# First block: the relative-bias table laid out outside the kernel and loaded once, in place of 64 one-hot products and seven copies

## The reference

```python
bias = rpb[:, dr[None, None, :, None], dc[:, :, None, :]].astype(jnp.float32)
s_loc = jnp.einsum('bjqhd,brjkhd->bhjqrk', qb, kb).astype(jnp.float32) + bias
s_loc = jnp.where(mask[:, :, None, :], s_loc, NEG_INF)
...
p = jax.nn.softmax(jnp.concatenate([s_loc, s_ctx], axis=-1), axis=-1)
```

## Time and profile before

| | us |
|---|---|
| median of 3 runs | 2392.49 |
| lowest, highest | 2392.35, 2395.34 |
| span of the profiled execution | 2394.4 |
| TensorE busy in it | 2212.5 (92%) |
| VectorE busy | 928.0 (39%) |
| ScalarE busy | 713.1 (30%) |
| GpSimd busy | 22.2 (1%) |

### The profile page before, as it was taken

The page is one execution under the profiler, slowest core; times in us unless marked ns, Lnnn a source line. Parts: engine busy times, 40 slices in busy tenths (PEclk is TensorE's granted clock), DMA queues, the critical chain, the costliest instruction groups (busy, mean ns, idle before and its releaser), DMA issues.

```text
span 2394.4 us, 33085 instructions
## 1 busy us (share of the span) xinstructions
PE 2212.5 (92%) x13876; PEld 1578.1 (66%) x13876; DVE 928.0 (39%) x1357; ACT 713.1 (30%) x953; POOL 22.2 (1%) x34
## 2 busy tenths in 40 slices
PE   6999988998898889888998899999999799999998
PEld 4888786333333333333333498997999689998997
DVE  3555575221111111111111365466344464574453
ACT  4123443211111111111111334444333444544432
POOL 0100010000000000000000000000000000000000
PEclk8899999999999999999999999999999899999998
DMA  9663335899999999999999734544544454443542
GB/s 351 231 209 107 103 100 172 363 427 428 427 428 428 428 427 428 427 428 423 429 426 428 289 143 150 165 153 141 176 159 142 150 169 141 160 157 141 176 156 92
DMA packets 137357, 626.99 MB, mean 262 GB/s; under 512 B 7719, under 2 KB 31799, under 8 KB 112375
## 3 DMA queue, kind: packets, MB, share of 16 engines
q1 hardware_dynamic: 128688, 605.67, 64.8%
q0 software_dynamic: 6272, 18.09, 2.6%
q10 hardware_dynamic: 2247, 1.01, 0.2%
HBM read 623.69 MB, written 1.05 MB: 261 GB/s over the span
## 4 chain that ended last, share of the span: by engine, by line
PE 69%; DMA 22%; DVE 4%; issue 3%; ACT 2%; ACTq 1%; DVEq 0%
DMA ring<-in_w_lin 20%; PE bank L1596 15%; PE bank L1685 12%; PE bank L1920 11%; PE bank L1935 5%; PE bank L1843 3%; PE bank L1316 3%; PE bank L1266 2%; PE bank L1862 1%; PE bank L1709 1%; DMA ring<-in_w_in 1%; PE bank L1251 1%; PE bank L1694 1%; PE bank L1463 1%; PE bank L1370 1%
## 5 line engine op out<-in xcount | busy, mean ns | idle before, releaser
L1596 PE MATMUL bank<-ring,arenaA 128*64 128x512 f32 x3072 | 692.9, 601 | 39.1 <-DMA ring<-in_w_lin 28.6
L1596 PEld LDWEIGHTS bank<-ring,arenaA 128*64 128x64 f32 x3072 | 211.0, 138 | 461.9 <-issue 389.9
L2472 DVE TENSOR_TENSOR ring_rounded<-ring,ring_rounded 128x2048 fp32r<-128x2048 f32 (+1 forms) x160 | 338.2, 2153 | 149.6 <-ACT ring_rounded L960 149.6
L960 ACT ACTIVATE ring_rounded<-ring 128x2048 fp32r<-128x2048 f32 (+1 forms) x160 | 280.3, 1799 | 282.0 <-DMA ring<-in_w_in 106.4
L1685 PE MATMUL bank<-arena_rounded,ring_rounded 128*128 128x256 f32 x2496 | 310.4, 284 | 0.0
L1685 PEld LDWEIGHTS bank<-arena_rounded,ring_rounded 128*128 128x128 f32 x2496 | 302.6, 191 | 4.1 <-issue 3.1
L1920 PE MATMUL bank<-arena_rounded,ring_rounded 128*128 128x256 f32 x2112 | 257.3, 283 | 0.7 <-DVE arena_rounded L2662 0.5
L1920 PEld LDWEIGHTS bank<-arena_rounded,ring_rounded 128*128 128x128 f32 x2112 | 254.4, 191 | 3.8 <-ACT arena_rounded L1102 2.8
L2418 DVE TENSOR_SCALAR arenaA<-bank 128x512 f32<-128x512 f32 x32 | 22.1, 692 | 502.8 <-PE bank L1596 502.8
L941 ACT ACTIVATE arenaA<-bank 128x512 f32<-128x512 f32 x32 | 19.1, 597 | 328.7 <-PE bank L1641 328.7
L1935 PE MATMUL bank<-arena_rounded,ring_rounded 128*128 128x256 f32 x912 | 109.9, 283 | 2.3 <-DVE arenaA L2674 2.3
(11 more groups left out here) (382 smaller groups left out, 2200.0 us busy)
## 6 DMA issues: line engine op xcount, KB each, us to landing
ring<-in_w_down SPq DMA_DIRECT2D x64, 2048.0 KB, 22.0
ring<-in_w_gate SPq DMA_DIRECT2D x64, 2048.0 KB, 23.0
ring<-in_w_lin SPq DMA_DIRECT2D x64, 2048.0 KB, 25.5
ring<-in_w_in SPq DMA_DIRECT2D x35, 2048.0 KB, 11.5
ring<-in_w_ffn_gate SPq DMA_DIRECT2D x10, 2048.0 KB, 7.8
ring<-in_w_ffn_up SPq DMA_DIRECT2D x10, 2048.0 KB, 7.7
ring<-in_w_ffn_down SPq DMA_DIRECT2D x12, 1536.0 KB, 6.4
arenaA<-in_w_ada POOLq DMA_DIRECT2D x16, 1024.0 KB, 5.8
```

The lines of the kernel that those rows point to most:

```text
L960: act.activation(place2(name + "_hi", ringR)[:, a:b, :], place2(name)[:, a:b, :], ACT.Copy).then_inc(w_hi, 1)
L1596: last = pe.matmul(bank[b][k * SLOTS:(k + 1) * SLOTS, :], lhsT(c), slot(j)[:, c % 4, k * 512:(k + 1) * 512], start=False, stop=(c == DC - ...
L2472: dve.tensor_tensor(place2(name, ringR)[:, a:b, :], w[:, a:b, :], hi[:, a:b, :], ALU.subtract).then_inc(w_lo, 1)
```

## The change

The table is laid out in full, 128 x 3072 numbers, from `rpb` by fixed indices before the launch, passed as the input `window_bias` in place of `rpb` and `rel`, and loaded by SP in one transfer right behind `nav`. The first `front` waits for it. The products, the copies, the matmuls at L1190, the load of `rpb` and their semaphores go. The list `slabs` is two entries shorter, so every later slab sits two slots further back in the ring, and the order in which expert 0's slabs are issued changes with it.

```diff
+def window_bias(rpb):
+    q = np.arange(GRID_W)[:, None]
+    kc = np.arange(GRID_W)[None, :]
+    first = np.clip(q - WIN_W // 2, 0, GRID_W - WIN_W)
+    inside = (kc >= first) & (kc < first + WIN_W)
+    column = np.where(inside, kc - q + WIN_W - 1, 2 * WIN_W - 1)
+    table = np.concatenate([rpb, np.full(rpb.shape[:2] + (1,), NEG, rpb.dtype)], axis=2)
+    halves = [table[:, 5 - a:11 - a, :][:, :, column] for a in range(2)]
+    return np.stack(halves).transpose(0, 3, 1, 2, 4).reshape(P, NA_H * 6 * GRID_W)
...
-                  ("rel0", A["rel"][:, 0:4096]), ("rel1", A["rel"][:, 4096:8192]),
                   ("mlk", half(C_MLK)), ("mlv", w_in[:, :, C_MLV:C_MLG]), ("mlv_hi", None), ("mlq", half(C_MLQ))]
...
-                dst = raw1(name) if len(src.shape) == 3 else ring[:, (n % RING) * SLAB:][:, 0:4096]
-                sp.dma_start(dst, src).then_inc(slab_in[n % RING], 16)
+                sp.dma_start(raw1(name), src).then_inc(slab_in[n % RING], 16)
+                if name == "nav":
+                    sp.dma_start(bias[:, :, :].rearrange("p a b -> p (a b)"), A["window_bias"]).then_inc(wbias_in, 16)
...
-            for j in (4, 5, 0, 1, 2, 3):
+            for j in (2, 3, 4, 5, 0, 1):
                 sp.wait_ge(*freed(N1 - RING + j))
                 expert_slab(0, j)
...
-            act.wait_ge(ones_set, 1)
-            act.dma_start(rpbrows[0:120, 31:62], A["rpb"][0].rearrange("h r d -> (h r) d")).then_inc(rpb_in, 16)
...
-            pe.wait_ge(rpb_in, 16)
-            for a in range(2):
-                last = pe.matmul(bank[7][0:62, 0:48], rpbrows[0:120, 31 - 31 * a:93 - 31 * a], ...)
-            last.then_inc(vecs_turned, 1)
...
-            def rel_group(b):
...
-                for k in range(10 * b, min(10 * b + 10, 64)):
...
-                    last = pe.matmul(bank[4 + b % 2][:, 48 * (k - 10 * b):48 * (k - 10 * b) + 48], sl[0:63, k % 32, :],
-                                     relrhs[0:63, :], start=True, stop=True)
-                last.then_inc(rel_done, 1)
...
-                pe.wait_ge(rel_copied, 7)
...
-            dve.wait_ge(vecs_turned, 3)
-            dve.tensor_copy(relrhs[0:62, :], bank[7][0:62, 0:48]).then_inc(relrhs_set, 1)
...
             ada_part(4, range(8))
-            ada_part(5, range(4))
-            rel_copy(0)
-            ada_part(5, range(4, 8))
+            ada_part(5, range(8))
             rest1("mlk")
-            rel_copy(1)
             modulation(4)
             ada_part(6, range(8))
-            rel_copy(2)
             modulation(5)
-            ada_part(7, range(4))
-            rel_copy(3)
-            ada_part(7, range(4, 8))
-            rel_copy(4)
+            ada_part(7, range(8))
             rest1("mlv")
             modulation(6)
-            rel_copy(5)
             ada_part(8, range(8))
-            rel_copy(6)
             modulation(7)
...
+                if i == 0:
+                    dve.wait_ge(wbias_in, 16)
```

More of the change, by code:

```diff
@@ L214, in build @@
         vin2 = small[:, 128:256]
-        relrhs = small[:, 256:304]
-        rpbrows = PT[:, 1, 0:93]
         lfb = small[:, 304:320]
@@ L458, in build @@
         out_done = sem("out_done")
-        ones_set = sem("ones_set")
         vecs_turned = sem("vecs_turned")
@@ L462, in build @@
         x_copied = sem("x_copied")
-        rpb_in = sem("rpb_in")
-        relrhs_set = sem("relrhs_set")
+        wbias_in = sem("wbias_in")
         bg_in = sem("bg_in")
-        rel_done = sem("rel_done")
-        rel_copied = sem("rel_copied")
         silu_done = sem("silu_done")
@@ L598, in freed @@
             name = slabs[n][0]
-            if name.startswith("rel"):
-                return rel_done, (4, 7)[int(name[3:])]
             last = {"nak": "na_k3", "nak_hi": "na_k3", "nav": "na_v3", "nav_hi": "na_v3", "mlk": "ml_k1", "mlv": "ml_v3",
@@ L1187, in _ @@
             ada_turn(0)
-            pe.wait_ge(rpb_in, 16)
-            for a in range(2):
-                last = pe.matmul(bank[7][0:62, 0:48], rpbrows[0:120, 31 - 31 * a:93 - 31 * a],
-                                 K["ident"][0:120, 0:120].rearrange("p (h r) -> p h r", r=15)[:, :, 5 - a:11 - a], start=(a == 0), stop=(a == 1))
-            last.then_inc(vecs_turned, 1)
             pe.wait_ge(par_copied, 1)
@@ L1216, in ada_fold @@
                 last.then_inc(lin_done, 1)
-            def rel_group(b):
[L1220 to L1223, removed]
-                for k in range(10 * b, min(10 * b + 10, 64)):
-                    if k in (0, 32):
-                        slab(f"rel{k // 32}")
-                    sl = ring[:, (S1[f"rel{k // 32}"] % RING) * SLAB:][:, 0:4096].rearrange("p (k q) -> p k q", k=32)
-                    last = pe.matmul(bank[4 + b % 2][:, 48 * (k - 10 * b):48 * (k - 10 * b) + 48], sl[0:63, k % 32, :],
-                                     relrhs[0:63, :], start=True, stop=True)
-                last.then_inc(rel_done, 1)
-            REL_AFTER = {"na_v0": 0, "na_v1": 1, "na_v2": 2, "na_v3": 3, "ml_k0": 4, "ml_k1": 5, "ml_v0": 6}
             bothHi = lambda c: hBoth[:, :, c, :]
@@ L1268, in tokens @@
                 last.then_inc(lin_done, 1)
-                if f"{nm}{t}" in REL_AFTER:
-                    rel_group(REL_AFTER[f"{nm}{t}"])
             def features(name, sname, cols, n=P):
@@ L1282, in features @@
                 last.then_inc(lin_done, 1)
-                if name in REL_AFTER:
-                    rel_group(REL_AFTER[name])
             for t in range(2):
@@ L1970, in link @@
                 dve.wait_ge(dve_chain, links[0])
-            dve.memset(relrhs[:, :], 1.0)
-            dve.memset(rpbrows, 0.0).then_inc(ones_set, 1)
             dve.memset(ones[:, :], 1.0)
@@ L2016, in _ @@
                                      op0=ALU.add, op1=ALU.mult).then_inc(gains_done, 1)
-            dve.memset(mlV[:, :, 128:129], 1.0).then_inc(ones_set, 1)
+            dve.memset(mlV[:, :, 128:129], 1.0)
             def rest1(name, pieces=None):
@@ L2728 @@
     arrays, aps = {}, {}
-    for name, a in list(inputs.items()) + list(constants().items()):
+    laid = dict(inputs)
+    laid["window_bias"] = window_bias(_np.asarray(laid.pop("rpb"))[0])
+    for name, a in list(laid.items()) + list(constants().items()):
         a = _np.ascontiguousarray(a)
```

## The result

The changed kernel takes 2363.15 us (median of 4 runs, 2361.63 to 2369.3) against 2393.61 us for the kernel before on the same chip (4 runs, 2392.35 to 2395.34). The ratio is 0.9878 with a 95% interval of 0.9866 to 0.989. Timed twice more, on the same chip as its comparison each time, it gave 0.9884 (0.9864 to 0.9904) and 0.9894 (0.9877 to 0.9911). The profiled execution of the changed kernel spans 2367.4 us, 27.0 us less than the earlier trace rows, and took 2369.3 us itself, the longest of its four.

A forecast was written before the change was run, and what follows sets the result against it. Bound: TensorE's unbroken chain of tiles from 74.83 to 160.83 us, with the load-paced expert stage tied to it. 15.2 + 9.5 + 0.8 = 25.5 us off the 2392.5 median gives 2367.0 us; range 2363 to 2374.

The forecast's parts named there:

- The products, 15.2 us: Seven groups of small matmuls at L1228, between TensorE's tiles, leave the chain with nothing in their place: 15.2 us less.
- The clock behind them, 9.5 us, with 0.8 on the folds: Six tiles behind product groups return to full clock, 9.5 us less; four folds save 0.8; products, not folds, cause dips.
- The rival that went by the Trainium skill: Dips in the tiles stay, brought by something other than the products; only 15.2 us go, 2377.3 us; chance 0.07.
- VectorE, 0: Seven copies leave VectorE, which must be ready 25 us sooner; at least 5 us of cover everywhere, so cost 0.
- The transfers, 0, with 4.1 us if nak is delayed: New table load behind nav delays neither nak nor nav, cost 0; rival with nak 4.1 us late, 2371 us, chance 0.05.
- The order of expert 0's slabs, 0: Expert 0's slabs load as 2, 3, 4, 5, 0, 1; w_gate, now last, has 16 us of cover or more, cost 0.
- The head, 0: L1190 matmuls, L2003 copy and ACT issue go before ScalarE's wait for nak ends at 42.10; gain 0, at most 0.8 us.
- What I couldn't lay out, plus or minus 3 us: Clock dips around the norms, 343 to 422 us, may shift: at most about 7 us, allowed plus or minus 3 us.

The follow-up runs named there:

- the split sums: Changed kernel with the 20 small gate-sum matmuls split in four pieces between halves of ml_o0 and ml_o1: 2363.65 us, then 2360.8 beside the changed kernel's 2366.71.

## Why the prediction was right

The forecast was 2367.0 us, 25.5 less; the medians say 26.5 to 30.5 less, the profile 27.0 over the span. The mechanism was right: the products, and the low clock behind them, both on the chain. The closeness of the sum is in part luck. It fits the stretch of tiles, 85.7 us before and 59.9 after, because it was read from the same execution; from the second profile of the kernel before it would have been 22.4. And 2363.15 lies only 0.15 us above the low end of the range.

- **The products, 15.2 us.** Shown: full matmuls of the same length cost 14.8 us in the tiles with no dip, and products alone give everything back.
- **The clock behind them, 9.5 us, with 0.8 on the folds.** Shown in kind, since the tiles run at 1.00 when the products are gone and dip when only they return. Not fixed in size: the second profile of the kernel before had three dips, 5.6 us in the tiles and 1.6 on the folds, and its stretch was 3.0 us shorter. My words that the products cause the dips and the folds don't were half right. A fold alone brings none; behind a group with a fold a dip came more often than behind a group without one (11 of 12 against 2 of 6). The rule of the Trainium skill, "TensorE: Matmul & The Clock Gate", section "HAM oscillation — how this bites in real kernels", asks for idle gaps, and none are recorded in these groups. The measurement decides: behind groups of 63 rows and 48 columns, with TensorE recorded 100% busy in them, the low level came in each of the four profiles that have them. The rival that went by the Trainium skill is refuted by the products put back, which bring the slow tiles back with them.
- **VectorE, 0.** Shown by the copies put back. The laid-out times held: mlv's rests at 106.3 against 106.8, ada 8 at 114.5 against 112.9, ada 9 at 125.6 against 122.3, the last two because the refills issued between 98.6 and 114.9 us took 6.8 to 9.1 us, not 5.8. The cover was thinnest at mlv's rests, 5.4 us ahead of ml_v0 at 111.7, and 8.6 us or more at each fold from ada 5 to ada 9.
- **The transfers, 0, with 4.1 us if nak is delayed.** The table landed at 50.9 us against some 51, nak wasn't delayed, and the load put first delayed nak by 3.7 us.
- **The order of expert 0's slabs, 0.** The last two were issued at 356.8 and 363.3 us, the slowest of the six took 16.3, and the first product at 396.36 waited for neither; the version with the old order and the longer ring was as fast.
- **The head, 0.** nak came 0.26 us sooner, and the first tile began when it did before.
- **What I couldn't lay out, plus or minus 3 us.** Here is what is left over. In the first pair of profiles the first score product came 27.6 us sooner: the gate sums ahead of it took 4.4 us at a granted clock of 1.00, where they had taken 6.1 at 0.70. By the first expert product 26.35 was left of it. The rest of the 30.5 us, up to 4, isn't located. The three timings put it between 0 and 4; the stretch behind the first expert product, the second block's loads among it, scatters by 8.7 us over the profiles, which is enough to hold it.

## What to carry to other kernels

Small matmuls cost their own time and may cost more in the full matmuls behind them, here 5.6 to 9.5 us on top of 15.2: read the granted clock in the window behind a stretch of small matmuls, not only in it, where it can still say 1.00. When such work can't go, try it in short pieces with no other small work next to them, which was followed by no dip in the pieces tried here (four of 1.5 to 1.8 us, and the split sums in two executions), or with all rows in use, which had one dip in six. And take the same windows from two profiles before a clock term goes into a sum with a decimal.

## What the hardware showed that I had not expected

- The clock's dips behind identical groups came six times in one execution of the kernel before (1.6 us each) and three times in another, one of which cost 2.4 us and 0.8 more on the fold ahead of it.
- Six groups of 20 instructions of 63 rows and 48 columns, 2.36 us each, were followed by three, four and six dips in three executions; with 128 rows, 2.16 us each, by one in the only execution. Whether it is the rows stays open.
- A 1.57 MB load moved from behind two 2 MB loads to ahead of them delayed the first of them by 3.7 us, 0.4 us less than its own length at the 386 GB/s of the earlier trace rows.
